# RWKV steps of a two-block kernel: a one-operation token shift, 32-blocks copied by ScalarE, and another order in the preparing steps

## The reference

```
def token_shift(f, mu):
    f_prev = jnp.pad(f, ((0, 0), (1, 0), (0, 0)))[:, :-1]
    return f + (f_prev - f) * mu

def step(state, inp):                       # scanned over the 512 tokens, 16 heads of 64
    r_t, w_t, k_t, v_t, kk_t, a_t = inp
    sa = jnp.einsum('bhij,bhj->bhi', state, -kk_t)
    state = (state * w_t[:, :, None, :] + sa[..., None] * (kk_t * a_t)[:, :, None, :]
             + v_t[..., None] * k_t[:, :, None, :])
    return state, jnp.einsum('bhij,bhj->bhi', state, r_t)
```

## Time and profile before

| | us |
|---|---|
| median of 3 runs | 1778.08 (1777.31 to 1779.62) |
| the profiled execution: its own time | 1778.84 |
| the profiled execution: span from the first to the last instruction | 1777.1 |
| PE busy | 1734.8 (98%) |
| DVE busy | 845.3 (48%) |
| ACT busy | 724.9 (41%) |

### The profile page before, as it was taken

The page is one execution under the profiler, slowest core; times in us unless marked ns, Lnnn a source line. Parts: engine busy times, 40 slices in busy tenths (PEclk is TensorE's granted clock), DMA queues, the critical chain, the costliest instruction groups (busy, mean ns, idle before and its releaser), DMA issues.

```text
span 1777.1 us, 22126 instructions
## 1 busy us (share of the span) xinstructions
PE 1734.8 (98%) x9338; PEld 1429.4 (80%) x9338; DVE 845.3 (48%) x1223; ACT 724.9 (41%) x1092; POOL 515.0 (29%) x129
## 2 busy tenths in 40 slices
PE   7999999999999999999999999999999999999997
PEld 6897778888887888888888888877778888888886
DVE  3015467998989854251133443527744411123343
ACT  5244544655556452352222223536653522222222
POOL 2442300000000003534444445332344244444442
PEclk9999999999999999999999999999999999999999
DMA  5432231010011124322222222322222222222221
GB/s 188 167 129 72 80 111 57 28 51 25 28 40 36 36 97 152 142 107 95 95 95 95 95 95 95 124 77 72 72 95 95 96 96 104 96 95 95 95 95 71
DMA packets 57093, 159.44 MB, mean 90 GB/s; under 512 B 3455, under 2 KB 35071, under 8 KB 42404
## 3 DMA queue, kind: packets, MB, share of 16 engines
q1 hardware_dynamic: 44556, 135.80, 22.1%
q10 hardware_dynamic: 12440, 22.24, 3.6%
HBM read 150.41 MB, written 9.19 MB: 90 GB/s over the span
## 4 chain that ended last, share of the span: by engine, by line
PE 88%; DVE 5%; ACT 4%; issue 1%; POOL 1%; DMA 0%; ACTq 0%; SPq 0%; DVEq 0%
PE ps L643 25%; PE ps L645 24%; PE ps L644 24%; PE ps L1093 2%; ACT ht_hi L1447 1%; PE ps L1081 1%; PE ps L1173 1%; PE ps L1135 1%; POOL w_lo L634 1%; PE ps L1101 1%; PE ps L1010 1%; PE ps L1125 1%; ACT w_hi L1412 1%; PE ps L1145 1%; PE ps L828 1%
## 5 line engine op out<-in xcount | busy, mean ns | idle before, releaser
L634 POOL TENSOR_TENSOR w_lo<-w_raw,w_hi 128x2048 fp32r<-128x2048 f32 (+2 forms) x125 | 514.7, 4123 | 1232.0 <-ACT w_hi L1412 1208.0
L643 PE MATMUL ps<-ht_hi,w_hi 128*128 128x512 f32 (+1 forms) x1312 | 525.3, 400 | 7.3 <-DVE ht_lo L2173 3.4
L645 PE MATMUL ps<-ht_hi,w_lo 128*128 128x512 f32 (+1 forms) x1312 | 499.6, 381 | 0.0
L644 PE MATMUL ps<-ht_lo,w_hi 128*128 128x512 f32 (+1 forms) x1312 | 498.8, 380 | 0.0
L1412 ACT ACTIVATE w_hi<-w_raw 128x2048 fp32r<-128x2048 f32 x125 | 239.2, 1914 | 453.9 <-PE ps L645 407.8
L643 PEld LDWEIGHTS ps<-ht_hi,w_hi 128*128 128x128 f32 x1312 | 247.7, 189 | 67.9 <-issue 17.7
L645 PEld LDWEIGHTS ps<-ht_hi,w_lo 128*128 128x128 f32 x1312 | 247.4, 189 | 48.7
L644 PEld LDWEIGHTS ps<-ht_lo,w_hi 128*128 128x128 f32 x1312 | 248.4, 189 | 39.5 <-issue 1.9
L2762 DVE TENSOR_TENSOR hid_lo<-hidden,hid_hi 128x1024 fp32r<-128x1024 f32 x27 | 129.3, 4788 | 149.1 <-ACT hid_hi L1988 149.1
L643 PE MATMUL ps<-w_hi,hid_hi 128*128 128x512 f32 x432 | 168.2, 389 | 0.0
L645 PE MATMUL ps<-w_hi,hid_lo 128*128 128x512 f32 x432 | 168.1, 389 | 0.0
(11 more groups left out here) (333 smaller groups left out, 2345.1 us busy)
## 6 DMA issues: line engine op xcount, KB each, us to landing
w_raw<-in_wpack SPq DMA_DIRECT2D x113, 1024.0 KB, 4.8
w_raw<-in_wpack SPq DMA_DIRECT2D x26, 512.0 KB, 5.1
x_res<-in_x SPq DMA_DIRECT2D x4, 512.0 KB, 7.2
gate_back<-gate_dram ACTq DMA_DIRECT2D x2, 1024.0 KB, 6.9
gate<-gate_dram ACTq DMA_DIRECT2D x1, 2048.0 KB, 8.2
x_res<-in_x ACTq DMA_DIRECT2D x1, 2048.0 KB, 7.7
out_x<-y_tok ACTq DMA_DIRECT2D x4, 512.0 KB, 4.0
bias_skewed_dram<-bias_rows_dram ACTq DMA_DIRECT2D x1, 1792.0 KB, 10.9
```

Of the source, the lines that this page charges most:

```text
L634: last = nc.gpsimd.tensor_tensor(Wl[:, slot, cc], raw[:, slot, cc], f32(Wh[:, slot, cc]), ALU.subtract)
L643: mm(dst, wh, ah, start=first, stop=False)
L644: mm(dst, wh, al, start=False, stop=False)
L645: return mm(dst, wl, ah, start=False, stop=last)
```

## The change

1. `shift_half` becomes one operation. The scaled copy that ACT writes stands one column to the right in a tile of 513 columns (half_tile) whose column 0 is set to zero once, so DVE makes all 512 tokens in one `scalar_tensor_tensor`.
2. The off-diagonal 32 x 32 blocks (level 5's result) are copied into `Wf` by ACT (`half_blocks`: four instructions for each k, one for each 32 partitions, each for the blocks of all four chunks) and no longer by DVE's `copy_predicated`. DVE's two products of level 6 now wait for ACT.
3. `first_step`: PE runs 5, 5, 4, 2 and 3 pieces around its five own operations (4, 4, 4, 3 and 4 before). ACT widens the keys ahead of the sigmoid of half 11 and the weights' DMAs. DVE takes the reciprocal ahead of the second clearing of the gram tiles and of the start of `Z`.
4. `second_step`: PE runs level 4's second product ahead of the two turns to tokens, with 4 pieces ahead of it and 2 behind (3 and 3 before). ACT copies level 4's result ahead of taking half 16. DVE does level 3's k = 1 ahead of `key_scale(1)`, and `decay_args(1)` ahead of the reciprocal.
5. Two tiles change places in memory: the second full inverse moves to where gate_tile was.

```diff
         RKV = r("rkv", [P, 2, 3, T])
-        GT = r("gate1_tile", [P, T])
+        tf_early = r("tinv_full1", [P, NT, P])
...
-        TF = [r(f"tinv_full{h}", [P, NT, P]) for h in range(2)]
+        TF = [r("tinv_full0", [P, NT, P]), tf_early]
+        GT = r("half_tile", [P, T + 1])
...
             def first_step():
 
-                advance(firsts, 4)
+                advance(firsts, 5)
                 pe.wait_ge(a1["out_taken"], 2)
                 key_sums(0)
-                advance(firsts, 4)
+                advance(firsts, 5)
                 key_roots(0)
                 advance(firsts, 4)
                 gate_z(-1, 0)
+                advance(firsts, 2)
+                bonus(0)
                 advance(firsts, 3)
-                bonus(0)
-                advance(firsts, 4)
...
                 level_x(0, 4)
-                advance(firsts, 3)
+                advance(firsts, 4)
+                level_t(0, 4)
                 to_tokens(0, 0)
                 to_tokens(0, 1)
-                level_t(0, 4)
-                advance(firsts, 3)
+                advance(firsts, 2)
                 key_roots(1)
...
+            def half_blocks(b, k):
+
+                w("tt_full", 2 * nl - 1, b, 2 * nl - 4 + k)
+                src = ps[:, (4, 6)[k], :].rearrange("p (t c) -> p t c", c=P)
+                for q in range(4):
+                    rows, cols = slice(32 * q, 32 * q + 32), slice(32 * (q ^ 1), 32 * (q ^ 1) + 32)
+                    ins = actf(Wf[k][rows, :, cols], src[rows, :, cols], ACT.Copy)
+                inc(ins, "whole_ready")
...
                 key_root(0)
+                widen_keys(0)
                 take_side(11)
                 lora_weights(1)
-                widen_keys(0)
...
                 exponentials(1)
+                half_blocks(0, 0)
+                half_blocks(0, 1)
                 weights_behind(17)
...
                 deviation(a)
+                if has_b:
+                    half_blocks(b, 0)
+                    half_blocks(b, 1)
                 widen_norm(a)
...
-                    shift(N_SHIFTED[n], RKV[:, pair % 2, part, :], 0, GT, 8 * part + pair)
+                    mu = 8 * part + pair
+                    dve.wait_ge(staged, N_SHIFTED[n])
+                    v.scalar_tensor_tensor(RKV[:, pair % 2, part, :], bank(half_bank(n)), OM[:, mu:mu + 1], GT[:, 0:T],
+                                           ALU.mult, ALU.add).then_inc(shifted, 1)
+                    dve.wait_ge(shifted, N_SHIFTED[n])
...
+                elif lv == nl - 1:
+                    w("whole_ready", 6, b, 3 + k)
+                    src = Wf[k][:]
                 else:
                     w("tt_full", 2 * nl - 1, b, max(2 * lv - 2 + k, 1))
                     src = b3((4, 6)[k])
-                if lv > 1:
-                    w("whole_ready", 4, b, 2)
+                if 1 < lv < nl - 1:
+                    w("whole_ready", 6, b, 2)
                     order(v.copy_predicated(Wf[k][:], blocks(lv - 1), src))
```

21 lines of the change are left out of this document (11 added, 10 removed).

## The result

The changed kernel takes 1786.65 us (median of 4 runs, 1785.05 to 1787.32) and the kernel before, beside it, 1777.93 (1777.31 to 1779.62): ratio 1.0043, 95% interval 1.0031 to 1.0055. It is slower by 0.4%, and its median lies 1.15 us above the forecast's range.

A forecast was written before the change was run, and what follows sets the result against it. PE, busy 50.66 of 51 us in a full step, was taken as the bound, so only its idle gaps could change the time. Terms of -1.5, -0.35 and +6.08 gave +4.2 us, a median of 1782.2, range 1778.5 to 1785.5.

The forecast's parts named there:

- the chain at level 6: Full steps: ACT's root, four k = 0 copies (1.15 us), DVE's product, PE's level 6, gram copies, next grams.
- Steps 0 to 4: Level 6 in five full steps: grams 0.81 us late each, waiting for ACT's copies behind the root; +4.05 us.
- if the copies start before the root: Sign of being wrong, full steps: ACT's copies were to start within 0.02 us of the root's end.
- Step(5): Level 6 there: saved shift column takes 0.16 us off first, then grams wait for ACT's copies; +0.25 us.
- step(6): Level 6 there: PE did not wait before; grams now wait for ACT's root and copies; +1.78 us.
- Second preparing step: Removed waits bring 2.0 us by level 5; ACT's copies at level 6 leave -0.35 us of it.
- First preparing step: Waits ahead of key_sums(0) and key_roots(0) go, 2.4 us gained, partly given back; -1.5 us, or -1.0 if the unit loads no earlier.
- The shift: Full steps, DVE: about 0.17 us saved on the single column only makes DVE wait longer for ACT's copies.
- The sum: Whole kernel: -1.5 - 0.35 + 6.08 = +4.2 us on the profiled span; median 1782.2 us, case 1, chance 0.50.
- the second case: Level 6, eight places: copies overlap, 0.19 us each, 0.85 for four; +1.8 us, 1779.9 us; chance 0.17.
- the third (copies of 0.39 us): Level 6, eight places: ACT's copies cost 0.39 us each whatever their length; +7.6 us, 1785.6 us; chance 0.13.
- the fourth (a first step that keeps its gain): First preparing step gives nothing back because half 13 or the weight unit stalls PE anew; +5.7, 1783.8 us; chance 0.12.

The follow-up runs named there:

- three profiles: Profiles of the unaltered changed kernel from three comparisons with the kernel before, on three chips; median times 1786.65, 1784.60 and 1784.29 us.
- level4_before: Changed kernel without ACT's 32-block copies, PE's and ACT's level 4 order in the second preparing step as in the kernel before: 1777.25 us, ratio 0.9987.
- late_clear: Changed kernel without ACT's 32-block copies, DVE's second clearing and scaled identity moved behind the queries in the first preparing step: 1776.82 us, ratio 0.9989.
- gate_copy_first: Changed kernel without ACT's 32-block copies; first step's gate copy before weight conversion, DVE's clearing and identity before queries, weight split behind keys: 1774.70 us.
- two later comparisons: The unaltered changed kernel measured again beside the kernel before on two other chips: 1784.60 and 1784.29 us, ratios 1.0033 and 1.0031.
- after_filled: Changed kernel with one PE piece moved ahead of level 6's first product in the second preparing step and steps 0 to 4: 1779.02 us, ratio 1.0000.
- blocks_in_five_steps: Changed kernel with ACT's 32-block copies in steps 0 to 4 alone, DVE copying those of pairs 0, 6 and 7: 1779.39 us, ratio 1.0004.
- blocks_only: Kernel before plus the 32-block copies by ACT alone, shift and orders as before: 1786.86 us, ratio 1.0039.
- shift_only: Kernel before plus the one-operation shift alone, with its zero column and the buffer move it needs: 1778.55 us, ratio 0.9996.

## Why the prediction was wrong

The direction and the chain at level 6 were right; the forecast failed by its size. The step that failed is the premise of the first paragraph: "PE's work is the same before and after, so the time can only change by PE's idle gaps and by what opens new ones". Each new idle time was counted at its own length and the clock at full throughout, at no price and without a reason. In the profiled execution 3.43 of the 7.43 us are not idle time but PE's same work at the lower clock: 1.55 behind the new idle time of the second preparing step and 1.88 at the start, where the code is the same and the change has no part in it. The range was built from prices of copies and had no term for either. What comes after the steps did move along, as forecast: from 685 us to the end the difference stays within 0.05 us.

- **Steps 0 to 4, forecast +4.05.** Measured +3.46 to +3.51 in three profiles, 0.70 a step. The copies' price was right to 0.01 us each. They begin 0.10 before the root's end (485.45 against 485.55), where I had them begin with it; that is the 0.11 a step. By the letter this met a sign of being wrong, "if the copies start before the root": they start after the root's start and before its end, and the chain is the same.
- **Step(5), +0.25, and step(6), +1.78.** +0.19 to +0.23 and, at full clock, +1.47 to +1.49. The wait ahead of step(6)'s level 6 is 1.06 and the grams' 0.25.
- **Second preparing step, -0.35.** -0.45 and -0.48 where the clock held. The gain until level 5 was 2.04 to 2.06 for the forecast 2.0, and level4_before shows that PE's and ACT's new place of level 4 brings 1.9 of it.
- **First preparing step, -1.5.** -0.75 to -0.77 in the three profiles of the changed kernel. The waits to go went. The mis-sized term is what is given back, and the trace shows why: DVE's `tensor_scalar` on the root, 0.17 us before, takes 0.89, and this stands on ACT's chain of root, widening, table load and exponentials. ACT began the weight unit at 229.03 - 1.88 = 227.15 on the old scale, where I had 226.5. late_clear shows that this chain and not DVE's queue sets `bonus(0)`, gate_copy_first that 1.8 us of it hang on the weight unit standing ahead of the gate's copy on ACT and of the keys on DVE, which it changes together.
- **The shift** was worth 0.11 a step, where DVE's saved time was forecast only to lengthen its wait. Both hold: with the copies behind the root it brings nothing, and without them 0.11.
- **The sum.** Without start and low clock the three profiles give 7.43 - 1.88 - 1.55 = 4.00, 4.44 - 0.45 = 3.99 and 5.47 - 1.55 = 3.92 us: the forecast's 4.2 is 0.2 off, where the first step's error of +0.75 and those of the steps of -0.85 nearly cancel. That the total of the terms came out so near is in that part luck. The low stretch's 1.55 is the second step's 1.10 + 0.45 in the first profile, and 3.04 - 1.49 in the third.
- **What the range missed.** In the first comparison +8.7 us of medians stand for 4.0 of terms. Its profile shows 1.88 before the attention and 1.55 in the second step, both at the lower clock; the other 1.3 is that the two profiled executions lie 0.91 above their median (1778.84, before) and 0.38 below it (1786.27). In the two later comparisons medians of +5.7 and +5.6 leave 1.6 to 1.7, about one low stretch. PE idles 1.04 to 1.20 us at level 6 eleven times in the profiles, and the clock fell behind it in 4: once in the six of the second step, three times in the five of step(6). It fell behind none of the waits of 0.74 to 0.77 in steps 0 to 4, and after_filled and blocks_in_five_steps, which have none over 1 us at level 6, come out where their marks put them (+0.1 us by medians for +0.45 without the start, +0.7 for +0.5).

Shown is that the copies cause the loss, that their place behind the root and the missing work on PE make the most of it, that stretches at the lower clock cost 1.55 to 3.2 us where a profile has one in the steps, and that all executions of the two kernels without the long idle times at level 6 stood at 0.998 or 0.999. Not shown is why low stretches follow some idle times and not others. The length of the wait alone does not decide it: the kernel before waits 1.57 us in its first preparing step and 1.19 ahead of level 4 in its second, late_clear 1.5 us twice, all at full clock, and so do blocks_only, shift_only and level4_before at the places that they share with the kernel before. Nor is it shown why all four runs of the first comparison stood at 0.996 or 0.997, and 8.7 us above the kernel before where the later ones stood 5.6 or 5.7; of the four only one has a trace.

Of the rivals the third (copies of 0.39 us) and the fourth (a first step that keeps its gain) come nearest the time, but neither occurred: the copies take 0.278, and the first step gave back more, not less. A range is not right because some wrong case reaches the number.

The Trainium skill (ScalarE: Activation LUTs, section What ACT_TABLE_LOAD costs) has neighbours overlap by about 93 ns. The 64 copies of the profile, 0.278 apart at 0.268 long, show no overlap, and that settles the second case as well.

## What to carry to other kernels

Moving work from a busy engine to an idle one costs what the new engine's queue puts ahead of it: here the copies were cheap, but they were behind a root that waits for something else, and the engine relieved just waited. If a wait on PE can't be removed, put independent work ahead of it: one piece moved took back 0.63 of 0.70 us in each step, at no cost in instructions. A sum of idle times needs one more term, for a clock that may fall behind a new one: here it fell in 4 of 11 cases behind new waits of over 1 us and behind no shorter one of the steps, so those places are the ones to test. And before two profiled spans are compared, their starts and their clocks have to be.

The version with the lowest time is gate_copy_first: new orders and the one-operation shift, 32-blocks by VectorE, and the gate's copy ahead of the weight unit, 1774.70 us against 1779.20 (0.9974, 0.9963 to 0.9985).

## What the runs showed of the hardware

- Granted clock: behind 1.19 + 0.25 us of idle PE it was 0.55 and 0.60 over 4 us and 1.00 after; in another execution of the same kernel, behind 1.17 + 0.25, it stayed 1.00. Blocks_only had 0.50 for six us and lost 3.2. Waits of 1.57 and 1.19 us in the kernel before were followed by 1.00.
- The first TENSOR_SCALAR of the first preparing step takes 0.4 to 0.7 us more than later ones, whichever it is: the scaled identity 0.92 and the root 0.17 in the old order, the root 0.89 and the identity 0.43 in the new. Where it stands on a chain it counts.
- A copy by ScalarE of 32 partitions by 128 columns costs about as much as one of 128 partitions by 128: 0.268 us and 0.278. Four for the blocks of 32 rows thus cost four times that.
- Executions of the same code differ before the attention begins, by -1.0 to +1.9 us in fifteen profiles against that of the kernel before, and the difference is carried to the end. In the two that differ most it goes with the time from which the matmuls run at the full rate: 12.8 us or earlier for -1.0, 21.3 for +1.9, 16.8 in the kernel before. A single profile's span is not a comparison.
